# Layer 1's output product in four parts, two of them inside the attention run, and the experts' norm token tile by token tile

## What is computed

```python
# layer 1 ("odd" layer), the last of the first block; h is 256 x 1024
y = concat([window_gqa(...), rms_norm(diff_attention(...), subln_g) * (1 - lam_init)], -1) @ w_out   # 256 x 1024 by 1024 x 1024
h = h + g1 * y
x = rms_norm(h, norm2_g) * (1 + sc2) + sh2
logits = x @ router                     # 8 experts, two of them chosen for each token
h = h + g2 * sum_e gates[:, e] * ((silu(x @ w1[e]) * (x @ w3[e])) @ w2[e])
```

## Time and profile before

| what | value |
|---|---|
| median of three runs | 1960.55 us (1958.65 to 1961.99) |
| the profiled execution's own time | 1962.71 us |
| span of its instructions | 1960.8 us |
| mean granted TensorE clock | 0.933 of 2.4 GHz |
| PE busy | 1764.6 us (90%) |
| DVE busy | 1251.0 us (64%) |
| ACT busy | 824.9 us (42%) |
| POOL busy | 134.4 us (7%) |
| HBM read | 329.96 MB, 169 GB/s over the span |

### The profile page before, as it was taken

One profiled execution on the slowest core, in us unless ns is written; L12 is line 12 of the kernel. 1 busy time (PEld: TensorE's weight loads), 2 busy tenths in 40 slices (PEclk: granted clock), 3 DMA queues, 4 the chain that ended last, 5 costly groups with the idle time before them and its releaser, 6 DMA issues. The chain is left out here.

```text
span 1960.8 us, 22044 instructions
## 1 busy us (share of the span) xinstructions
PE 1764.6 (90%) x8958; PEld 1480.0 (75%) x8958; DVE 1251.0 (64%) x1709; ACT 824.9 (42%) x999; POOL 134.4 (7%) x128
## 2 busy tenths in 40 slices
PE   4897998899799997799779999999988988889998
PEld 1774786788677886788667888888868856768987
DVE  5355685467645553575648888898886545565644
ACT  5322232422112223333326776777744433535542
POOL 1230000200020011230010000000030000000000
PEclk8896997999999998889779999999998979898999
DMA  7431332255544541211047888888855521135553
GB/s 289 110 108 65 129 130 88 84 194 178 182 187 173 201 148 67 96 52 55 11 150 272 320 319 321 316 326 326 329 207 173 190 67 52 65 129 183 174 193 128
DMA packets 61437, 332.59 MB, mean 170 GB/s; under 512 B 16836, under 2 KB 17411, under 8 KB 28178
## 3 DMA queue, kind: packets, MB, share of 16 engines
q1 hardware_dynamic: 56080, 321.54, 45.4%
q10 hardware_dynamic: 4354, 6.32, 1.0%
q0 software_dynamic: 896, 3.26, 0.5%
HBM read 329.96 MB, written 1.13 MB: 169 GB/s over the span
## 5 line engine op out<-in xcount | busy, mean ns | idle before, releaser
L1957 DVE TENSOR_TENSOR wlo__65<-raw__64,whi__66 128x2048 fp32r<-128x2048 f32 (+2 forms) x68 | 157.0, 2309 | 117.0 <-ACT whi__66 L1443 117.0
L1957 DVE TENSOR_TENSOR wlo__61<-raw__60,whi__62 128x2048 fp32r<-128x2048 f32 (+3 forms) x56 | 125.4, 2239 | 83.6 <-ACT whi__62 L1443 83.6
L1443 ACT ACTIVATE whi__66<-raw__64 128x2048 fp32r<-128x2048 f32 (+2 forms) x68 | 127.1, 1869 | 122.7 <-DMA raw__64<-in_ffn_w 49.8
L1957 DVE TENSOR_TENSOR wlo__69<-raw__68,whi__70 128x2048 fp32r<-128x2048 f32 (+4 forms) x52 | 110.2, 2118 | 42.8 <-ACT whi__70 L1443 42.7
L1443 ACT ACTIVATE whi__62<-raw__60 128x2048 fp32r<-128x2048 f32 (+3 forms) x56 | 102.9, 1837 | 73.5 <-DMA raw__60<-in_ev_w_in 22.1
L1443 ACT ACTIVATE whi__70<-raw__68 128x2048 fp32r<-128x2048 f32 (+4 forms) x52 | 90.4, 1739 | 30.3 <-DMA raw__68<-in_w_ff 11.1
L1990 DVE SCALAR_TENSOR_TENSOR wsum__71<-raw__68,silu_rows 128x1024 f32<-128x1024 f32 x84 | 99.9, 1220 | 3.5 <-DMA raw__68<-in_ada_w 3.0
L2953 POOL TENSOR_TENSOR keep__58<-keep__58,keep__59 128x1 f32<-128x1 f32 (+3 forms) x48 | 49.2, 1027 | 632.3 <-DVE keep__58 L2029 632.3
L2212 DVE TENSOR_REDUCE keep__58<-ps 128x1 f32<-128x256 f32 (+1 forms) x104 | 56.6, 544 | 27.7 <-PE ps L891 20.9
L1443 ACT ACTIVATE whi__139<-raw__137 128x2048 fp32r<-128x2048 f32 (+2 forms) x15 | 26.2, 1744 | 108.9 <-DMA raw__137<-in_ffn_w 108.9
L1957 DVE TENSOR_TENSOR wlo__138<-raw__137,whi__139 128x2048 fp32r<-128x2048 f32 (+2 forms) x15 | 31.2, 2079 | 55.2 <-ACT whi__139 L1443 55.2
(11 more groups left out here) (1095 smaller groups left out, 5446.9 us busy)
## 6 DMA issues: line engine op xcount, KB each, us to landing
raw__68<-in_ada_w SPq DMA_DIRECT2D x26, 1024.0 KB, 5.0
raw__64<-in_moe_w SPq DMA_DIRECT2D x24, 1024.0 KB, 6.3
raw__60<-in_moe_w SPq DMA_DIRECT2D x24, 1024.0 KB, 6.6
raw__68<-in_moe_w SPq DMA_DIRECT2D x16, 1024.0 KB, 5.8
raw__226<-in_moe_w SPq DMA_DIRECT2D x16, 1024.0 KB, 5.1
raw__230<-in_moe_w SPq DMA_DIRECT2D x16, 1024.0 KB, 6.1
raw__60<-in_ada_w SPq DMA_DIRECT2D x15, 1024.0 KB, 6.1
raw__64<-in_ffn_w SPq DMA_DIRECT2D x13, 1024.0 KB, 5.0
```

Source lines behind the costliest of these rows:

```text
L1443: e.activation(t.hi(), t.raw(), ACT.Copy).then_inc(*did("hi", i))
L1957: e.tensor_tensor(t.lo(), t.raw(), t.hi().bitcast(F32), ALU.subtract).then_inc(*did("lo", i))
```

## The change

The output product is made in the order A, B, C, D. A and B need only `CQ3`, and become steps of the filling generator: 8 steps each (A's in steps 24 to 27 of the run, two in each; B's in steps 28 and 29, four in each). C and D follow the run and add to the same four PSUM banks. Behind the product, DVE's and POOL's programs go token tile by token tile: gate, mean and scale of token tile 0, then the same of token tile 1, and POOL's power of tile 0 ahead of its last addition. The scaled rows and ACT's squares are written over rows of h that are no longer used (`h_t[2:4]`, the context's), not into an area of their own. PE makes the 8 transposes of token tile 0, then the 8 of token tile 1, into banks 4 to 7. Calls of `feed` and the points where `ahead` rises to 2 are moved, and with them the weights' splits.

The diff, cut to its core, in the order SBUF, step table, `paired` and the rest of PE's program, ACT's, DVE's, POOL's:

```diff
-    XSm = M.some(2, 1024)
+    XSm = h_t[2:4]
...
-    HEADS["a1"].filled = [min(160, 40 + 8 * i) for i in range(40)]
+    HEADS["a1"].filled = [min(160, 40 + 8 * i) + min(max(2 * (i - 23), 0), 8) + min(max(4 * (i - 27), 0), 8) for i in range(40)]
...
+            for half in range(2):
+                tile, hi, lo = use(W["od_w_out"][0][0:512, half * 512:half * 512 + 512], 4, 512)
+                for t in range(2):
+                    take("4" if half else "c", "o", 1, half, t)
+                for t in range(2):
+                    for k in range(4):
+                        for s, n in state["due"](*fin_done("a1", t)):
+                            e.wait_ge(s, n)
+                        m = mm3(bank("o", 1, half, t), sub(CQ3, slice(None), k, slice(t * 128, (t + 1) * 128)),
+                                sub((hi, lo), slice(None), k), k == 0, False)
+                        if (t, k) == (1, 3):
+                            m.then_inc(*done("part", "o", 1, half))
+                            consumed(tile, "part", "o", 1, half)
+                        yield
...
-            proj(("o", 1, half), y1, 2, KT, W["od_w_out"][0][:, half * 512:half * 512 + 512], 512,
-                 lambda t, k: fin_done("a1", t if k < 4 else 2 + t), "6")
+            tile, hi, lo = use(W["od_w_out"][0][512:1024, half * 512:half * 512 + 512], 4, 512)
+            for t in range(2):
+                for k in range(4):
+                    for s, n in due(*fin_done("a1", 2 + t)):
+                        e.wait_ge(s, n)
+                    m = mm3(bank("o", 1, half, t), sub(DQ3, slice(None), k, slice(t * 128, (t + 1) * 128)),
+                            sub((hi, lo), slice(None), k), False, k == 3)
+                m.then_inc(*done("prod", "o", 1, half, t))
+            consumed(tile, "prod", "o", 1, half, 1)
...
-            b = take("6", "mt", k0)
...
+            take("y", "mt", k0)
+        for t in range(2):
+            for k in range(KT):
+                for s, n in due(("mxn", t)):
+                    e.wait_ge(s, n)
+                o = k % 2 * 256 + t * 128
+                m = tr(bank("mt", k - k % 2)[:, o:o + 128], XSm[t][:, k * 128:(k + 1) * 128])
+                if k % 2 and t:
+                    m.then_inc(*done("mt", k - 1))
...
         attend("a1", paired)
+        for t in range(2):
+            feed(("prod", "o", 1, 0, t))
         at["ahead"] = 2
-        for half in range(2):
-            for t in range(2):
-                feed(("prod", "o", 1, half, t))
...
-        at["ahead"] = 2
         for half in range(2):
+            if half:
+                at["ahead"] = 2
+                gain("n2b", sc2b, 0, 8, 9)
             for t in range(2):
-                feed(("prod", "o", 1, half, t))
+                if not half:
+                    feed(("prod", "o", 1, half, t))
                 gated(("o", 1), half, t, bank("o", 1, half, t), GBC[:, half * 512:half * 512 + 512],
...
+                if half:
+                    means("mms", (t,), SS[:, t:t + 1], D, ("msq", t))
+                    for s, n in due(("mrs", t)):
+                        e.wait_ge(s, n)
+                    e.tensor_scalar(XSm[t], h_t[t], SS[:, t:t + 1], None, ALU.mult).then_inc(*did("mxn", t))
...
                 residual(("o", 1), half, t, HEADS["a1"].p[half * 2 + t])
-        for t in range(2):
-            rsqrt("mrs", (t,), SS[:, t:t + 1], ("mms", t))
+                if half:
+                    rsqrt("mrs", (t,), SS[:, t:t + 1], ("mms", t))
```

More of the change, by code:

```diff
@@ L2554, in vector_program @@
                 empties(("o", 1, half, t), ("rt", ("o", 1), half, t))
-        gain("n2b", sc2b, 0, 8, 9)
-        for t in range(2):
-            means("mms", (t,), SS[:, t:t + 1], D, ("msq", t))
-            for s, n in due(("mrs", t)):
-                e.wait_ge(s, n)
-            e.tensor_scalar(XSm[t], h_t[t], SS[:, t:t + 1], None, ALU.mult).then_inc(*did("mxn", t))
+                if half:
[3 more added lines that the diff above has]
+                    e.tensor_scalar(XSm[t], h_t[t], SS[:, t:t + 1], None, ALU.mult).then_inc(*did("mxn", t))
         for k0 in (0, 4):
```

9 lines of the change are left out of this document (1 added, 8 removed).

## The result

The changed kernel took **1943.22 us** (median of 6 runs, 1939.90 to 1947.73) beside 1960.10 for the kernel before (6 runs, 1956.96 to 1961.99): a ratio of 0.9914, interval 0.9901 to 0.9927. Two repeats gave 1946.96 and 1946.37. All 19 runs of it have a mean of 1945.7 us (standard error 1.0; numbers behind a ± are standard errors too) and 86 runs of the kernel before, from all series of this case, one of 1959.4 (0.4). So the gain is nearer to 13.7 ± 1.0 us than to 16.9, and still more than forecast. The profiled execution took 1947.73 us, span 1945.8.

The account below looks back on a forecast made before the run. PE bounds the experts' loop; ahead of it a chain of small dependent steps sets the end. Gains of 8.1 us up to the output product's end and 1.6 behind sum to 9.7: 1960.55 to 1950.9 us, range 1948.4 to 1955.5.

Parts of the forecast that it names:

- Step 24, free: Ahead of unit 20's values product: 6 filling matmuls, 1.4 us, and the transposes fit into PE's 2.38 us wait, costing nothing.
- Step 25, the level: Unit 20's values, 6 fillings, transposes and unit 21's values, 960.8 to 966.5; PE's clock low until 963.9, two fillings slow.
- high throughout: Rival: PE's clock stays high between 958 and 985, so the gain is 10.9 us, time 1949.7; chance 0.20.
- the forecast case: PE's clock low until 963.9, then high: output product ends 8.1 us earlier; 1949.9 to 1952 us overall, chance 0.45.
- The last norm covered by B, and no wait of D: B's 5.6 us fills PE's 4.15 us norm wait, overrunning by 1.5; D's weights are split by 982.6, before D starts.
- C behind the split of slot 60: C's first matmul comes within 0.2 us of the end of DVE's split of slot 60, at about 978.0.
- T at 989.4: T, the output product's end, comes at 989.4 instead of 997.49, 8.1 us earlier.
- T to top two, 1.6 us: From the output product's end to DVE's top two: 18.6 us instead of 20.2, by reordered gates, transposes and splits.
- Low for longer: Rival: PE's clock stays low through steps 25 to 27, gain only 5.5 us, time 1955.1; chance 0.26.
- Slower than before: Rival: fillings keep all of A to D at the low clock, about 17 us against 9.7, time 1968; chance 0.05.
- given back: Rival: transfers bound the experts' loop from its start, so an earlier start is useless, time 1960; chance 0.04.
- A start that is earlier by x ends it earlier by x: Experts' loop from 1035 us: PE, busy 358 of 365 us, bounds it, so an earlier start carries fully to its end.

Follow-up runs that it names:

- the run with the long delay: Kernel after the change plus two repeated DVE low-part operations (704 and 512 columns, 1.42 us of delay) ahead of the top two: 1946.07 us, ratio 0.9923.

## Why the prediction was right or wrong

- **Step 24, free:** right. The wait ahead of unit 20's values is 0.84 us, not zero.
- **Step 25, the level:** here the first part of the error lies. It was taken low up to 963.9, as at the same time before; it was high throughout (the values 1.16 us from 959.08, the fillings 0.23 apart). The text priced this as a rival (*high throughout*, gain 10.9) and gave it 0.20; the local stretch gives 11.06. The run with the long delay shows the forecast case as well, so it was a real one, but the rarer. The reason wasn't missed, only its weight: the prediction says itself that the idle time shrinks to 1.0 us, and the level was high in all 12 profiles where it did (0.81 to 1.07 us).
- **The last norm covered by B, and no wait of D:** right. Filling B is worth 5.1 us by the run that takes it back.
- **C behind the split of slot 60:** right; 0.14 us behind its end (975.00), 0.2 allowed.
- **T at 989.4:** 986.58; of the 2.8 us, 1.7 lie ahead of the reduce, and 1.1 is step 25. Gain ahead of T 9.2, forecast 8.1.
- **T to top two, 1.6 us:** 1.84. The second gate 2.0 us behind its product (2.1 said), the copies 2.0 us behind the router's end (2.3 said), T + 18.37 (18.6 said): each link holds, and undoing the two waits gave 1.7 and 2.0 us. The router had 6.96 us (6.83 taken).
- **Low for longer:** fell. In the kernel after, 958 to 972 holds 12 transposes, the values and fillings at clock 1.00. The rule of the Trainium skill that spoke for it (TensorE: Matmul & The Clock Gate, Part 4: PE-mode transpose) doesn't decide here: mixed with 512-column matmuls, transposes did not bring the level down, nor did 16 of them behind the added matmuls. Behind T the level did fall after 2.24 us of idle time and 8 transposes, which leaves open whether these counted.
- **Slower than before, given back:** neither came. The experts' loop is as it was (from 1025 to 1390 us PE is busy 358.6 of 365).
- **"A start that is earlier by x ends it earlier by x", and nothing rounded in "for side effects":** this is the step that failed. In the experts' loop it holds to within 2 us (by 300 us behind its start, the profiles with the same instructions lie at most that far apart), and not in the stages behind it: from the experts' first matmul to the end the same instructions took between 922 and 931 us. The kernel before stood at the long end in both of its profiles. By the means, 13.7 ± 1.0 were gained, 11.06 of them in the local stretch. The other 2.6 ± 1.0 lie outside of it, where the prediction had nothing. The profiles point to the stages behind (930.8 and 931.0 before, 928.5, 924.7 and 924.7 after), above all to one low spell of PE's clock 540 to 560 us behind the experts' start, which was short in two of the three profiles of after and long in both of before. But the time up to the reduce scatters by up to 6.5 us too, so how much of the 2.6 came from where isn't shown, nor is what sets the spell's length.
- **The range:** it had 1.3 us for the median's scatter, taken from three runs (1958.65 to 1961.99). The 86 runs spread from 1947.5 to 1965.8, and the first six of the kernel after lay 2.4 us below the mean of its 19, by luck. Without that luck the time is still below the range. Together, from 1950.9 to 1943.2: 1.1 for the base (1960.55, where the mean of the 86 is 1959.4), 1.4 for the local chain, 2.6 outside of it and 2.5 between the six runs' median and the mean of all, 0.1 being rounding.

## What to carry to other kernels

Filling in PE's waits pays twice, once as cover and once by holding the clock's level: cost the stretch at both levels, and look at what the wait becomes (here about 1 us went with the high level, 2.3 and more with the low one). A local chain can be foretold and measured to tenths of a microsecond between two instructions of a profile, and that is the place to judge an edit; the whole time of a program with many short waits around the edit can go several microseconds either way, from one execution to the next too, so a range needs that as a term of its own, taken from more than three runs. Where an edit moves a chain ahead, look for what it now stands behind on its own queue: the two waits found so in the prediction were worth another 3.9 us.

## What the runs showed of the hardware

- One unchanged program had executions from 1947.5 to 1965.8 us (86 runs), and a delay of 0.8 us on DVE went with a mean that was 2.2 ± 0.7 us lower. The same instructions behind a common point took 922 to 931 us; the largest part, 5.5 to 5.9 us, is one low spell 540 to 560 us behind that point.
- PE can be busy without a gap and stay at the low level for long: behind a wait of 6.24 us, the matmuls from 1575.98 to 1590.26 in the kernel before all ran at it (0.43 us apart, granted clock 0.50), and in the repeat of the kernel after the same ones were at the high level from 1562.94 on, 2.8 us behind their start.
- PE's product behind a wait of 0.81 to 1.07 us ran at the high level (1.16 us, 12 profiles), behind one of 2.30 to 2.43 us at the low one (1.88 to 2.08 us, 6 profiles).
- 32 fp32 router matmuls of 8 columns took 3.77 us at the high level and 6.96 at the low one, 8 transposes 1.06 and 1.97: these matmuls of few columns are as much slower at the low level (1.85 times) as those of 512 columns (0.43 to 0.233 us apart).
- With matmuls that nobody reads, the 16 transposes behind T ran at the high level in two nearly equal kernels; behind the router the level fell in both, though PE was kept busy, and only in one of them was it back for all of the gathers.
- A scalar_tensor_tensor of 8 columns on DVE, with both tensors in SBUF, took 0.16 us in the kernel after, and 0.85 us in the kernel with filling only, where POOL's 1.26 us addition was running beside it: it ended at 988.66, with the addition (988.63). The gate of 987.21, which reads one input from PSUM, kept its 0.68 us beside it. The Trainium skill (SBUF — State Buffer, the section SBUF: two separate sides) says that a DVE instruction with two inputs in SBUF and a GpSimd instruction that reads SBUF need the same pair of ports, that the first to start holds it for the whole instruction, and that the other is blocked until then; the rows agree. DVE's in the kernel after, DVE's with filling only, and POOL's there:

```profile
981.63 0.16 DVE L2089 SCALAR_TENSOR_TENSOR keep__52<-keep__52,keep__51 128x8 f32<-128x8 f32 x1
```

```profile
987.81 0.85 DVE L2091 SCALAR_TENSOR_TENSOR keep__52<-keep__52,keep__51 128x8 f32<-128x8 f32 x1
```

```profile
987.37 1.26 POOL L2984 TENSOR_TENSOR keep__50<-keep__50,odd__185 128x512 f32<-128x512 f32 x1 [4.11 <-DVE odd__185 L2286]
```
